# Attention stage of a two-layer trunk: gated chunks first, mask added by TensorE, compressed scores merged, eight identity transposes per unit

## The reference

```python
z = rms_norm(x, g) @ w_in
c_val, c_gate, q, k_c, v_c, k_s, v_s, k_w, v_w, g_log = split(z)
u = c_val * sigmoid(c_gate)                  # 512 channels
y = causal depthwise conv(u, 31 taps) + b    # then LayerNorm of groups of 64 channels, swish
# attention: 8 heads of 64, 2 KV heads, q and k normalised
kc, vc = compress(k_c), compress(v_c)        # 15 blocks of 32 tokens: silu(blk @ w1 + b1) @ w2 + b2
p_c = masked_softmax(q @ kc.T);  o_cmp = p_c @ vc
o_sel, o_win = masked softmax over all causal keys of k_s, k_w, times v_s, v_w
o = sigmoid(g_log) gates times (o_cmp, o_sel, o_win)
x = x + concat(conv_out, o) @ w_out
x = x + swiglu(rms_norm(x))                  # layer 0: dense, 2816 wide; layer 1: top 2 of 8 experts, 3584 wide
```

## Time and profile before

| | |
|---|---|
| median of three runs | 1653.21 us (1651.16 to 1655.38) |
| profiled execution | 1654.8 us, its span 1652.8 us |
| PE busy | 1563.0 us (95%) |
| DVE busy | 1211.1 us (73%) |
| ACT busy | 911.5 us (55%) |
| mean granted TensorE clock | 0.957 |
| attention stage of layer 0 | 0 to about 220 us |
| dense stage | about 220 to 420 us |
| attention stage of layer 1 | about 420 to 630 us |
| routing and expert loop | about 630 to 1653 us |

### The profile page before, as it was taken

One profiled execution on the slowest core, in us unless ns is written; L12 is line 12 of the kernel. 1 busy time (PEld: TensorE's weight loads), 2 busy tenths in 40 slices (PEclk: granted clock), 3 DMA queues, 4 the chain that ended last, 5 costly groups with the idle time before them and its releaser, 6 DMA issues.

```text
span 1652.8 us, 19780 instructions
## 1 busy us (share of the span) xinstructions
PE 1563.0 (95%) x7336; PEld 1233.4 (75%) x7336; DVE 1211.1 (73%) x1186; ACT 911.5 (55%) x834; POOL 24.3 (1%) x41
## 2 busy tenths in 40 slices
PE   6968899998896888999999999999999999999998
PEld 4654389998665437888888888888888888888886
DVE  2876254453287624888987988987988987989896
ACT  1024233432102424677777777777777677777674
POOL 1010000000001000000000000000000000000000
PEclk9977899999997788999999999999999999999999
DMA  8500086541551003999999999999999998999992
GB/s 291 180 2 1 0 286 205 189 161 53 202 181 51 1 0 136 356 367 371 361 359 332 365 368 371 361 359 334 361 371 372 360 365 328 359 372 365 363 364 102
DMA packets 199396, 426.57 MB, mean 258 GB/s; under 512 B 7314, under 2 KB 40338, under 8 KB 199316
## 3 DMA queue, kind: packets, MB, share of 16 engines
q1 hardware_dynamic: 198000, 424.89, 71.4%
q10 hardware_dynamic: 1316, 0.49, 0.1%
HBM read 424.31 MB, written 1.05 MB: 257 GB/s over the span
## 4 chain that ended last, share of the span: by engine, by line
PE 89%; DVE 7%; issue 2%; ACT 2%; DMA 1%; ACTq 0%; POOL 0%; POOLq 0%; DVEq 0%
PE bank L1387 13%; PE bank L1389 12%; PE bank L1388 12%; PE bank L1094 8%; PE bank L1411 6%; PE bank L1409 6%; PE bank L1410 6%; PE bank L1290 3%; PE bank L1289 3%; PE bank L1288 3%; PE bank L1268 3%; PE bank L1227 2%; PE bank L1137 2%; PE bank L1397 1%; PE bank L1186 1%
## 5 line engine op out<-in xcount | busy, mean ns | idle before, releaser
L717 DVE TENSOR_TENSOR w_lo<-ring,w_hi 128x2048 fp32r<-128x2048 f32 x369 | 843.1, 2291 | 184.3 <-ACT w_hi L471 183.8
L471 ACT CAST w_hi<-ring 128x2048 fp32r<-128x2048 f32 x369 | 705.4, 1914 | 268.3 <-PE bank L1389 165.3
L1387 PE MATMUL bank<-w_hi,xe_hi 128*128 128x512 f32 x896 | 355.2, 396 | 7.4 <-DVE w_lo L717 7.4
L1389 PE MATMUL bank<-w_hi,xe_lo 128*128 128x512 f32 x896 | 350.1, 391 | 0.0
L1388 PE MATMUL bank<-w_lo,xe_hi 128*128 128x512 f32 x896 | 349.7, 390 | 0.0
L1387 PEld LDWEIGHTS bank<-w_hi,xe_hi 128*128 128x128 f32 x896 | 168.7, 188 | 43.0 <-DVE w_lo L717 9.6
L1389 PEld LDWEIGHTS bank<-w_hi,xe_lo 128*128 128x128 f32 x896 | 168.6, 188 | 35.9
L1388 PEld LDWEIGHTS bank<-w_lo,xe_hi 128*128 128x128 f32 x896 | 168.9, 188 | 33.2
L1409 PE MATMUL bank<-w_hi,actT_hi 128*128 128x512 f32 x448 | 175.1, 391 | 0.0
L1410 PE MATMUL bank<-w_lo,actT_hi 128*128 128x512 f32 x448 | 174.5, 389 | 0.0
L1411 PE MATMUL bank<-w_hi,actT_lo 128*128 128x512 f32 x448 | 174.4, 389 | 0.0
(11 more groups left out here) (224 smaller groups left out, 1472.7 us busy)
## 6 DMA issues: line engine op xcount, KB each, us to landing
ring<-in_moe_w SPq DMA_DIRECT2D x336, 1024.0 KB, 6.1
ring<-in_dense_w SPq DMA_DIRECT2D x33, 1024.0 KB, 5.4
ring<-in_w_in SPq DMA_DIRECT2D x8, 2048.0 KB, 10.3
ring<-in_w_out SPq DMA_DIRECT2D x4, 2048.0 KB, 9.0
ring<-in_cmp_k_w SPq DMA_DIRECT2D x2, 2048.0 KB, 19.2
ring<-in_cmp_v_w SPq DMA_DIRECT2D x2, 2048.0 KB, 8.7
ring<-in_w_in SPq DMA_DIRECT2D x2, 1120.0 KB, 11.4
x_sb<-in_x SPq DMA_DIRECT2D x2, 512.0 KB, 5.1
```

What stands on the lines that cost most here:

```text
L471: nc.scalar.copy(w_hi[t % SPLIT][:], raw(t)).then_inc(w_hi_ready, 1)
L717: V.tensor_tensor(w_lo[t % SPLIT][:], raw(t), w_hi[t % SPLIT][:].bitcast(F32), ALU.subtract).then_inc(w_lo_ready, 1)
L1387: T.matmul(dst, xe_hi[:, kk, own], hi[:, k, :], start=(kk == 0), stop=False)
L1389: last = T.matmul(dst, xe_lo[:, kk, own], hi[:, k, :], start=False, stop=(kk == KD - 1))
```

## The change

In words:

- *Order of transfers*: `win 0` and `win 1` come first, `win 3` behind them. Their first halves (256 of 512 columns, enough for chunks 0 and 1) are transferred ahead of their second halves, with semaphores of their own.
- *Order on PE*: chunks 0 and 1, `z_product(0, i)`, chunk 2, transposes of `zdup`, chunk 3. ACT and DVE follow. Nearly all taps of the convolution are placed before the scores.
- q is transposed per token block and k per branch, into banks 7, 5, 2, 3, as each is ready.
- *Compressed scores*: `kcT` holds the keys of both KV heads in blocks with zeros elsewhere, so that one product gives both heads; they stand before the scores of unit 0, and their softmax is done between units instead of before them, in fewer DVE operations.
- *Mask*: an fp32r product of the identity with the causal mask is the first of the group that accumulates the scores. DVE takes the maximum from PSUM, ACT reads the scores there too, so `score(n)` waits for the exponentials of unit n-2.
- *Eight identity transposes* (`keep_busy`) before the wait for `p_ready` in every unit from the third.
- The compressed probabilities are transposed after unit 1, the means of the convolution after unit 2.
- In the dense stage `dact_hi` and `dact_lo` have two buffers.

```diff
-        stream += [("win", l, 3), ("win", l, 0), ("win", l, 1), ("cmp", l, 0), ("cmp", l, 1), ("win", l, 2), ("win", l, 4)]
+        stream += [("win", l, 0), ("win", l, 1), ("win", l, 3), ("cmp", l, 0), ("cmp", l, 1), ("win", l, 2), ("win", l, 4)]
...
+                if key in halved:
+                    sp.dma_start(dst[:, :, 0:S], src[:, :, 0:S]).then_inc(glu_arrived[0], 16)
+                    if key[2] == 1:
+                        for c in range(2):
+                            sp.dma_start(view("win", key[1], c)[:, :, S:BANK],
+                                         source("win", key[1], c)[0][:, :, S:BANK]).then_inc(glu_arrived[1], 16)
...
-                                             scores[:, n % 2, h * keys:(h + 1) * keys], ACT.Exp,
+                                             bank[n % 2][:, h * keys:(h + 1) * keys], ACT.Exp,
...
-                            if g >= 2:
-                                sc.wait_ge(w_used, piece_of["d2", 0, g - 2] + 1)
+                            if g >= 3:
+                                sc.wait_ge(w_used, piece_of["d2", 0, g - 3] + 1)
...
-                conv_taps(2, range(TAP_A))
+                conv_taps(2, range(22))
                 square_sums_q(0)
-                conv_taps(2, range(TAP_A, TAP_B))
+                conv_taps(2, range(22, 26))
+                normalised_q(0)
...
-                    link(V.tensor_tensor(s3, bank[n % 2][:].rearrange("p (h k) -> p h k", h=nh),
-                                         causal[:, 2 * P - keys:].unsqueeze(1).to_broadcast([P, nh, keys]), ALU.add))
-                    V.tensor_reduce(negmax[:, n % 2, 0:nh], s3, AX_X, ALU.max, negate=True).then_inc(s_ready, 1)
+                    V.tensor_reduce(negmax[:, n % 2, 0:nh], bank[n % 2][:].rearrange("p (h k) -> p h k", h=nh),
+                                    AX_X, ALU.max, negate=True).then_inc(s_ready, 1)
...
                 masked_scores(0)
+                compressed_scores()
                 masked_scores(1)
-                conv_taps(2, range(TAP_C, TAPS))
...
+                    if n == 0:
+                        compressed_probs()
...
                 for c in range(CC):
-                    if c == 0:
-                        wait_slot(pe, "win", l, 0)
-                        wait_slot(pe, "win", l, 1)
+                    if c % 2 == 0:
+                        pe.wait_ge(glu_arrived[c // 2], 32 * (l + 1))
+                    if c == 2:
+                        for i in range(NT):
+                            z_product(0, i)
...
+                        last = T.matmul(bank[6][:, o:o + KV * CPAD], qT[:, g, i * P:(i + 1) * P], kcT[:],
+                                        start=True, stop=True)
...
                     if n >= 2:
-                        pe.wait_ge(s_ready, NU * l + n - 1)
+                        pe.wait_ge(exp_ready, exp_count(l, n - 2))
                     r = slice(kv * HD, (kv + 1) * HD)
+                    T.matmul(bank[n % 2][:], ident_r[:],
+                             causal_r[:, 2 * P - keys:].unsqueeze(1).to_broadcast([P, nh, keys]),
+                             start=True, stop=False)
...
-                    pe.wait_ge(p_ready, NU * l + n + 1)
                     if n >= 2:
                         pe.wait_ge(pT_ready, NU * l + n - 1)
+                        keep_busy(2 + n % 2, 8)
+                    pe.wait_ge(p_ready, NU * l + n + 1)
```

More of the change, by code:

```diff
@@ L78, in hymba_trunk @@
     slot_of = {key: n for n, key in enumerate(slots)}
+    halved = [key for key in slots if key[0] == "win" and key[2] < 2]
+    turn_of = {key: len([o for o in slots[:n + 1] if o not in halved and slot_of[o] % SLOTS == n % SLOTS])
+               for n, key in enumerate(slots)}
     piece_of = {key: n for n, key in enumerate(pieces)}
@@ L207, in hymba_trunk @@
         x_loaded, par_loaded = sem("x_loaded"), sem("par_loaded")
+        glu_arrived = [sem(f"glu{h}_arrived") for h in range(2)]
         slot_arrived = [sem(f"slot{s}_arrived") for s in range(SLOTS)]
@@ L746, in _ @@
                 link(V.memset(blkT[:], 0.0))
+                glu(0)
+                glu(1)
+                dv.wait_ge(u_ready, CC * l + 2)
+                conv_taps(0, range(16))
                 for i in range(NT):
@@ L796, in _ @@
                 V.tensor_copy(kcn[0:MC, 1, :], kcn[0:MC, 0, :]).then_inc(kcn_ready, 1)
+                conv_taps(2, range(26, 29))
+                normalised_q(1)
                 dv.wait_ge(kcT_psum, l + 1)
[L798 to L811, removed]
+                for kv in range(KV):
+                    r, c = slice(kv * HD, (kv + 1) * HD), slice(kv * CPAD, kv * CPAD + NCMP)
+                    V.tensor_scalar(kcT[r, c], bank[4][r, c], par[r, l, col["k_g"]:col["k_g"] + 1], None,
+                                    ALU.mult).then_inc(kcT_ready, 1)
+                finished_q(0, 7)
                 for i in range(NT):
@@ L817, in _ @@
                 V.tensor_scalar(stat[:, 20:24], stat[:, 20:24], 1.0 / HD, EPS, ALU.mult, ALU.add).then_inc(stat_ready, 1)
-                conv_taps(2, range(TAP_B, TAP_C))
+                finished_q(1, 5)
+                finished_k(0)
                 dv.wait_ge(rstat_ready, 3 * l + 3)
@@ L1229, in values, with transpose_cp @@
                     last.then_inc(o_psum, 1)
[L1232 to L1238 removed]
+                def transpose_cp():
+                    pe.wait_ge(cp_ready, l + 1)
+                    for i in range(NT):
+                        for g in range(G):
+                            last = T.transpose(bank[6 + i][0:2 * CPAD, g * P:(g + 1) * P],
+                                               cp[:, i, g].rearrange("p k c -> p (k c)"), ident[:])
+                    last.then_inc(cpT_psum, 1)
+                    pe.wait_ge(cpT_ready, NT * (l + 1))
                 for n in range(NU):
@@ L1303, in down @@
                                     dst, r = bank[2 * n + i][:], slice(i * P, (i + 1) * P)
-                                    T.matmul(dst, dact_hi[:, f, r], hi[:, f, c], start=first, stop=False)
-                                    T.matmul(dst, dact_hi[:, f, r], lo[:, f, c], start=False, stop=False)
-                                    last = T.matmul(dst, dact_lo[:, f, r], hi[:, f, c], start=False, stop=end)
+                                    T.matmul(dst, dact_hi[:, g % 2, f, r], hi[:, f, c], start=first, stop=False)
+                                    T.matmul(dst, dact_hi[:, g % 2, f, r], lo[:, f, c], start=False, stop=False)
+                                    last = T.matmul(dst, dact_lo[:, g % 2, f, r], hi[:, f, c], start=False, stop=end)
                         last.then_inc(w_used, 1)
```

189 lines of the change are left out of this document (100 added, 89 removed).

## The result

The changed kernel took **1642.79 us** (median of 7, 1642.08 to 1647.67); the kernel before, on the same chip, 1654.62 us. The ratio is 0.9937, with an interval of 0.9927 to 0.9948. That is 11.8 us less where 34.4 were forecast, and 1.8 us above the upper end of the range (1641). The profiled execution has a span of 1640.9 us against 1652.8, 11.9 us less, so it can be laid beside the forecast place by place.

The account below looks back on a forecast made before the run. PE was taken as busy nearly everywhere, alternating with DVE and ACT in the attention stages, where the clock falls. From 1654.8 us, 27.6 (attention, two layers) and 6.8 (dense stage) were subtracted: 1620.4 us, range 1610 to 1641.

Parts of the forecast that it names:

- the first one: Expert loop behind 660 us: untouched by the diff, held at its 994 us, so gains lie only in attention and dense stages.
- the four rivals: Other outcomes: alternating clock 0.13 half way, 0.09 in full; 1.2 GHz throughout 0.06; late loads or late join 0.17 together.
- what would make the prediction wrong: Listed signs: clock 0.50 during identity transposes, PE waiting for exponentials from unit 4, scores after 108 us, expert loop length changed.
- Chunks first, and the moved DMAs: Front of attention stage: taps lie beside PE's work, moved loads cost 0.6 us per layer, scores start at about 106.1 us.
- Rival (c): Second compression matrix and `win 2` late, PE waiting 3 us for each per layer: 1632 us; chance 0.17 together with Rival (d).
- Rival (d): Join before the scores: they start at 110 us instead of 106, 1628 us; chance 0.17 together with Rival (c).
- The units: Attention units, bound by PE: output projection starts at 172.4 us instead of 186.2, 13.8 us per layer, 27.6 for both.
- the higher level until the last unit: Attention units: clock expected to rise by 128 us and stay at the higher level, held up by the identity transposes.
- Rival (a): Attention units: clock keeps alternating at 0.77, no gain there, 1648 us (chance 0.09); half way, 0.88, 1633 us (0.13).
- rival (b): Attention units: identity transposes do not hold the clock, PE at 1.2 GHz from 122 us, 1696 us; chance 0.06.
- rests on: Attention units: the forecast depends on the higher clock; eight transposes cost 9.1 us a layer; slower below a mean of about 0.73.
- The dense stage: Its last piece: two `dact_hi` buffers end it at 412.8 instead of 419.6, 6.8 us; 4.7 if the clock falls.

## Why the prediction was right, and where it was wrong

**The step that failed is the first one**: "The diff touches nothing behind 660 us (the expert loop, 60% of the time)", held at 994 us. It took 1017.9. The diff changes no instruction there, but new tiles ahead of the others moved one operand of each expert product by 64 bytes modulo 256, and 4032 products became 5.8 ns longer each. None of the four rivals contained this; what would make the prediction wrong did name it ("if the expert loop ... changes its length"), without a price. So 23.7 of the 35.6 us that the rest of the kernel gained were lost again. The loss is shown from both sides: put into the kernel before (+20.3 us) and taken out of the changed one (-21.5). With the distance restored the kernel takes 1621.25 us against the forecast of 1620.4; why the hardware has this pitch stays open.

**Chunks first, and the moved DMAs.** The scores started at 104.1, not 106.1. The second compression matrix was issued at 58.69 rather than 60.3, took 8.31 us and cost PE 0.80 (forecast 0.6). The 1.6 us earlier fit the clock, which the forecast did not consider here. From 16 to 39 us PE now has no gap and is at 1.00; the window of the changed kernel, then of the one before:

```profile
16.00:39.00 23.00, 23.00 (x83) 16.18 (x82) 9.20 (x24) 2.63 (x4) 0.00 (x0) 1.00 0.67 224
```

```profile
16.00:39.00 23.00, 22.93 (x69) 13.30 (x70) 2.63 (x4) 2.75 (x4) 0.00 (x0) 0.93 0.88 298
```

The start of the scores is no sharp test, though, since it varies between 102.7 and 107.7 us in the traces. Rival (c), late loads, is out: 0.80 us is PE's longest wait for a transfer between the first chunk and the scores, in both layers. Rival (d), a late join at 110 us, is out with 104.1.

**The units.** The projection began at 172.80 (forecast 172.4). That this is so near is luck, for two errors cancel: the scores started 2 us earlier, and the last values took 7.9 us instead of 4.4, since PE waits 1.33 us for ACT just before them and the clock falls. From the first scores to the projection it took 68.7 us in layer 0 and 66.2 in layer 1, where 66 were forecast for both; in layer 1 the last values took 6.3. PE did not wait for ACT's exponentials from unit 4 on: besides those 1.33 it waited once from 122 us to the projection, 0.74 us for DVE. The forecast had written "the higher level until the last unit", and priced those values at that level nonetheless.

**The clock.** Rival (a), the alternating clock, and rival (b), 1.2 GHz throughout, are out for this kernel: 1.00 from 132 to 163 us, and 0.95 from 530 to 565 in layer 1. The rule in the Trainium skill, page "TensorE: Matmul & The Clock Gate", Part 4 (PE-mode transpose), that such transposes don't count as PE-busy in the same way, is not what this case shows: between 147 and 163 us the clock is 1.00 with the transposes and 0.77 without. But the forecast took from its rows that the clock is what the gain "rests on". It is not. Without the transposes the kernel is as fast: the 9.1 us a layer that they were priced at, less 4.3 us between 147 and 163 in which PE would wait anyway, are by this estimate about what the lower clock costs there (16 us at 0.77 instead of 1.00 are 3.7). The 13 to 15 us per layer (172.80 or 171.32 instead of 186.21) come from the rest of the change: the mask off DVE, the taps done early, the merged compressed scores. These were not tried one by one, and how the gain divides among them stays open.

**The dense stage.** Forecast 6.8 us, measured 7.8 both in the trace and by taking the buffer away (1650.61 - 1642.79). The mechanism is as told. By the traces part of it is again placement: from the projection of layer 0 to the last dense product it takes 233.4 us in the kernel before, 225.7 in the changed one, and 226.6 in the changed one with its distances restored, so that the buffer is worth 6.8 us at equal placement and 6.2 by the kernel without it (231.8). The pitches give somewhat less for the placement: at the new distance the 1056 short products gain 2.2 us (120.0 to 117.9 ns), and the 264 long ones lose 264 x 6 ns = 1.6 us.

## What to carry to other kernels

A diff changes more than its lines: a new tile moves all that are allocated behind it, and in a kernel bound by TensorE the distance between the starts of the two operands can take back two thirds of what a change gains (23.7 of 35.6 us here). So compare the number of products per microsecond in a stage that was not touched; if it differs at equal clock and no waits, compare the addresses first and restore the distances with an unread tile. Filler that keeps the clock up is paid in the engine's own time: put it where the engine waits and right ahead of the work that gains (here the last values), not evenly into every step.

## What the runs showed of the hardware that was not expected

The pitch of back-to-back fp32r products of 512 columns at 2.4 GHz depends on the distance, modulo 256 bytes, between the starts of the stationary and the moving operand in their partitions: 227.7 ns at 0, 233.5 at 64, 232.4 at 128, 228.9 at 192. It holds with all other engines idle. In products of 256 columns the sign is turned, 119.5 ns at 0 and 118.7 at 128 alone; in the dense stage 120.0 with the placement of the kernel before and 117.9 with its tiles moved by 64. In these the weights are stationary, in those of 512 columns they move, and whether the columns or the roles turn the sign was not tried. Plain float32 products of 512 columns (429.1 ns) don't depend on it at the four distances tried. Why this is so was not found; the starts 16 bytes apart, which form no clean levels, fit no simple rule that was tried.
